# Keeping the residual in memory during the experts, so that its buffer can serve the weight ring

## The reference, cut to what matters

```
x  = x + g1 * mixer(...)                         # the residual, 128-row tiles
h2 = modulate(rmsnorm(x, norm_ffn_g), sh2, sc2)  # the second norm
f  = hier_moe(h2)    # per row 2 of 32 experts: (silu(h @ w1[e]) * (h @ w3[e])) @ w2[e]
x  = x + g2 * f
```

## Time and profile before

| | us |
|---|---|
| median of 3 runs | 2064.95 (2058.71 to 2065.15) |
| the profiled execution, time | 2062.01 |
| its span | 2060.2 |
| PE busy | 1904.3 (92%) |
| in the chain that ended last: PE, DMA | 66%, 22% |
| DMA RG<-in_moe_w in that chain | 20% |
| mean rate over the span | 287 GB/s |

### The profile page before, as it was taken

One profiled execution on the slowest core, in us unless ns is written; L12 is line 12 of the kernel. 1 busy time (PEld: TensorE's weight loads), 2 busy tenths in 40 slices (PEclk: granted clock), 3 DMA queues, 4 the chain that ended last, 5 costly groups with the idle time before them and its releaser, 6 DMA issues.

```text
span 2060.2 us, 35307 instructions
## 1 busy us (share of the span) xinstructions
PE 1904.3 (92%) x15271; PEld 1238.8 (60%) x15271; DVE 764.3 (37%) x1664; ACT 356.4 (17%) x795; POOL 307.4 (15%) x256
## 2 busy tenths in 40 slices
PE   6988999999999989999899888888789989999998
PEld 3565565555556548646555444444369779775884
DVE  1334382222222235315421111111157537647752
ACT  3132420000000012114210000000020130132231
POOL 0134411000000000116210000000000060040120
PEclk9999999999999999999999999999999999999999
DMA  9695399999999989318499999999975424417221
GB/s 331 174 330 216 106 392 389 427 427 426 427 425 424 426 336 308 109 41 318 169 371 427 426 427 426 426 426 425 420 283 179 144 80 164 145 61 205 83 94 61
DMA packets 136115, 591.02 MB, mean 287 GB/s; under 512 B 19410, under 2 KB 35818, under 8 KB 111248
## 3 DMA queue, kind: packets, MB, share of 16 engines
q1 hardware_dynamic: 119536, 564.45, 69.6%
q10 hardware_dynamic: 10304, 17.83, 2.8%
q0 software_dynamic: 6112, 6.39, 0.9%
HBM read 576.95 MB, written 25.33 MB: 292 GB/s over the span
## 4 chain that ended last, share of the span: by engine, by line
PE 66%; DMA 22%; DVE 5%; issue 3%; POOL 2%; ACT 2%; ACTq 0%; SPq 0%; DVEq 0%; POOLq 0%
DMA RG<-in_moe_w 20%; PE banks L1725 13%; PE banks L1007 7%; PE banks L1750 6%; PE banks L1270 4%; PE banks L1701 4%; PE banks L1010 4%; PE banks L2405 3%; PE banks L3093 3%; PE banks L3311 3%; PE banks L2862 2%; PE banks L720 2%; POOL AR L965 2%; PE banks L662 1%; PE banks L2864 1%
## 5 line engine op out<-in xcount | busy, mean ns | idle before, releaser
L1725 PE MATMUL banks<-RG,HT 128*64 128x256 f32 x3616 | 426.4, 389 | 38.5 <-DMA RG<-in_moe_w 36.2
L1725 PEld LDWEIGHTS banks<-RG,HT 128*64 128x64 f32 x3616 | 251.8, 134 | 224.8 <-DMA RG<-in_moe_w 60.2
L1734 DVE TENSOR_TENSOR AR<-AR,banks 128x256 f32<-128x256 f32 x64 | 38.6, 603 | 481.6 <-ACT AR L1730 430.4
L2004 POOL DMA_INDIRECT y_rows<-AR x64 | 63.7, 995 | 839.9 <-DVE AR L1764 811.7
L1750 PE MATMUL banks<-RG,AR 128*64 128x512 f32 x752 | 171.7, 598 | 3.8 <-DVE AR L1743 3.1
L1730 ACT ACTIVATE AR<-banks 128x256 f32<-128x256 f32 x64 | 24.5, 383 | 744.9 <-PE banks L1725 744.9
L1701 PE MATMUL banks<-AR 128*128 128x256 bf16 (+1 forms) x1152 | 149.4, 277 | 2.0 <-DVE AR L1689 1.5
L1701 PEld LDWEIGHTS banks<-AR 128*128 128x128 bf16 x1152 | 108.5, 98 | 33.6 <-issue 18.3
L1750 PEld LDWEIGHTS banks<-RG,AR 128*64 128x64 f32 x752 | 49.9, 136 | 94.4 <-issue 83.5
L1270 PE MATMUL banks<-RG,HT 128*128 128x512 f32 x192 | 84.8, 602 | 4.8 <-DVE AR L413 3.0
L965 POOL TENSOR_SCALAR AR<-AR,ST 128x768 f32<-128x768 f32 (+1 forms) x24 | 44.9, 1883 | 276.5 <-DVE ST L943 276.2
(11 more groups left out here) (508 smaller groups left out, 2766.3 us busy)
## 6 DMA issues: line engine op xcount, KB each, us to landing
RG<-in_moe_w SPq DMA_DIRECT2D x160, 2048.0 KB
AR<-in_moe_w SPq DMA_DIRECT2D x32, 2048.0 KB, 14.4
RG<-in_ada_w SPq DMA_DIRECT2D x24, 2048.0 KB
RG<-in_attn_w_in SPq DMA_DIRECT2D x20, 2048.0 KB
RG<-in_odd_w_in SPq DMA_DIRECT2D x6, 2048.0 KB
RG<-in_ssm_w_in SPq DMA_DIRECT2D x4, 2048.0 KB
AR<-y_rows SPq DMA_DIRECT2D x12, 512.0 KB, 6.2
RG<-in_even_w_out SPq DMA_DIRECT2D x2, 2048.0 KB
```

The source lines that it names most:

```text
L1725: m = pe.matmul(p[64 * h:64 * h + 64, 256 * i:256 * i + 256], x[:, k, :], w[:, h, k], start=k == 0, stop=k == 7, skip_group_check=True)
L2004: g.indirect_dma_start(y, off, E.Y[b], None, bounds_check=2047, oob_is_err=False).then_inc(*event)
```

## The change

- ACT stores each residual tile to a new DRAM tensor `x_rows` right behind the root of its second norm (`act_x_store`): four stores of 512 KB in layer 0, two in layer 1.
- `XS` becomes slot NS + 2 (7) of the ring. Before its first use in a layer SP waits for the last x store to have landed and for the last half of the norm.
- Slots are always put back, so slot 6 is used all through layer 1's experts. It enters as the second slot there and SP waits for the end of the attention and the second norm's gains before its first use.
- The order of the slots becomes 1, 2, 3, 4, 0, 7, 5 in layer 0 (seven) and 2, 6, 3, 4, 0, 7, 1, 5 in layer 1 (eight). Slot 7 is taken out when expert 30 is entered.
- Behind the issue of w2 of expert 31 SP waits for slot 7's last user and loads the residual back (`sp_x_back`), four or two loads of 512 KB. DVE's first `dve_last` waits for the last of them.
- `GATE1` moves from `XS` tile 3 to the small buffer `SVT`.

```diff
-    "mods_store0": ("x_loads",),
+    "mods_store0": ("x_loads", "x_back"),
...
+        XD = nc.dram_tensor("x_rows", [2, 512, D], F).ap()
...
-        extra = [None, ar(6 * KK, 4096)]
+        extra = [None, ar(6 * KK, 4096), XS[:].rearrange("p a b -> p (a b)")]
...
             slot = free.popleft()
-            if slot <= NS:
-                free.append(slot)
+            free.append(slot)
...
             extra[0] = ar((13, 11)[l] * KK, 4096)
-            free.insert(5, NS)
+            free.append(NS)
+            free.insert(5 - l, NS + 2)
             if l == 1:
-                free.insert(5, NS + 1)
+                free.insert(1, NS + 1)
...
+                if e == 30:
+                    free.remove(NS + 2)
...
+        def act_x_store(act, E, t):
+            act.dma_start(XD[E.l, 128 * t:128 * t + 128], XS[:, t, :]).then_inc(*dm("x_store", E.l, t))
+
+        def sp_x_back(sp, E, ended):
+            sp.wait_ge(*at(*ended))
+            for t in range(E.nt):
+                sp.dma_start(XS[:, t, :], XD[E.l, 128 * t:128 * t + 128]).then_inc(*dm("x_back", E.l, t))
...
                 act_root(act, (E.name, t), at_=t)
+                act_x_store(act, E, t)
                 act.wait_ge(*at(norm_end(E.name, t), E.name, t))
...
             act_root(act, (E.name, last), at_=last)
+            act_x_store(act, E, last)
             act_store_split(act, E, last - 1)
...
             v.wait_ge(*at("last_out", E.l, t))
+            if t == 0:
+                v.wait_ge(*at("x_back", E.l, E.nt - 1))
...
+                if slot >= NS + 1 and (key[1], slot) not in begun:
+                    l = key[1]
+                    begun.append((l, slot))
+                    if slot == NS + 1:
+                        sp.wait_ge(*at("att_out", "odd", 15))
+                        sp.wait_ge(*at("ada_scale", 1, 0))
+                    else:
+                        sp.wait_ge(*at("x_store", l, (3, 1)[l]))
+                        sp.wait_ge(*at("normed_half", (E0, E1)[l].name, (3, 1)[l], 1))
...
                 before[slot] = ended
+                if key[0] == "w2" and key[2] == 31:
+                    sp_x_back(sp, (E0, E1)[key[1]], before[NS + 2])
```

More of the change, by code:

```diff
@@ L298, in build @@
                 piece(("w2", l, e), down_source(W[2][e]), 4, 1024, ("down", l, x))
-            over_slots[l] = list(free)
+            over_slots[l] = [slot for slot in free if slot <= NS]
             free.remove(NS)
@@ L351, in build @@
                  ((4, 0, 0), (3, 0, 1), (4, 1, 2), (3, 1, 3), (2, 1, 5), (2, 0, 6), (5, 0, 7), (5, 1, 8))}
-        mods1 = {(2, 0): XS[:, 2, :], (5, 0): XS[:, 3, :], (3, 0): HT[:, 0:4, 256:512], (4, 0): HT[:, 4:8, 256:512]}
+        mods1 = {(2, 0): XS[:, 2, :], (5, 0): SVF[:, 0:512], (3, 0): HT[:, 0:4, 256:512], (4, 0): HT[:, 4:8, 256:512]}
         AB1 = SVF[:, 0:512].rearrange("p (a b) -> p a b", a=4)
@@ L2177, in sp_overflow @@
             last = where[("w2", l, 31)][2]
-            ended = {ring[i][3]: ring[i][4] for i in range(last - 5, last + 1)}
+            ended = {ring[i][3]: ring[i][4] for i in range(last - 11, last + 1)}
             W = [I[w][l].rearrange("e (p k) n -> e p k n", p=128) for w in ("moe_w1", "moe_w3")]
@@ L2569, in build @@
         FG, PG1 = ar(20 * KK, D), ar(21 * KK, D)
-        GATE1 = XS[:, 3, 0:512]
+        GATE1 = mods1[(5, 0)]
         def act_final_loads(act, e):
```

## The result

The changed kernel takes 2051.0 us (6 runs, 2047.8 to 2052.0) against 2061.1 us for the kernel before in the same sitting (6 runs, 2058.4 to 2065.2): ratio 0.9948, 95% interval 0.9935 to 0.9962. Two more sittings with the same two kernels gave 0.9975 (0.9962 to 0.9989) and 0.9973 (0.9960 to 0.9986), with 12 runs of the changed kernel and 35 of the one before each. The plain mean of the three ratios is 0.9965, some 7 us. Only the first of the three is a gain of over 0.3%.

The account below looks back on a forecast made before the run. The prediction took the weight stream to bound both expert stages; 3.9 us in layer 0 plus 4.3 in layer 1 gave 8.2, taking the median from 2065.0 to 2056.8 us, with an 8-in-10 range of 2051.5 to 2064.

Parts of the forecast that it names:

- The stream bounds both expert stages: Both layers' experts: each stage ends when the stream of 96 weight pieces ends, at about 426 GB/s.
- Layer 0, 3.9 us: Layer 0's experts: slot 7 closes two pauses, 4.5 us, less 0.6 for stores; below PE's 6.6 us of waits.
- Layer 1, 4.3 us: Layer 1: early piece and eight slots gain 4.3 us (3.3 to 4.9), with the x store landing after 11.1 us.
- one us for each us of later landing: Layer 1, SP before slot 7: each us the x store lands beyond 11.1 us costs one us.
- 4.9 us off the stream: Layer 1, before expert 0: slot 6's piece, issued at about 985 us, flows while nothing else does, saving 4.9 us.
- The way back, cost 0: Behind expert 31's w2: the residual's loads land 3 us before DVE needs them in layer 0; cost 0, at most 2 us.
- The traffic's cost: Stores beside the weights: the last x store costs 0.6 us in layer 0 and 1.2 us in layer 1.
- The number, 2056.8: Whole kernel: 8.2 us off the earlier runs' median of 2065.0 gives 2056.8 us.
- A: Layer 0: its lead is lost because PE bounds it, only layer 1's 4.3 us count; 2060.7 us, chance 0.17.
- B: Both layers: all twelve added transfers are paid in the stream, 14.8 us, net 3.1 us slower; 2068.1 us, chance 0.10.
- C: Layer 1: SP stands before slot 7 for the x store; gain gone at 19 us landing, 2072.7 at 27; chance 0.05.
- D: Start of layer 0's experts: more slots also bridge rate dips, gain above the sum; 2052 us, chance 0.06.

Follow-up runs that it names:

- slot6_only: Changed kernel without slot 7 and its stores, waits and loads in either layer; slot 6 still second and kept in layer 1; ratio 1.0006 to the kernel before.
- slot1_first: Changed kernel with slot 1 ahead of slot 7 in layer 1; ratios 0.9961 and 0.9967 to the kernel before.
- slot6_late: Changed kernel with slot 6 behind slot 7 instead of second in layer 1; ratio 0.9979 to the kernel before.
- layer0_only: Changed kernel with slot 7, its stores and loads in layer 0 alone, layer 1's ring as before the change; ratio 0.9979 to the kernel before.
- traffic_only: Kernel before's ring plus only the residual's stores and loads back, no slot 7, slot 6 for one piece; ratio 0.9997 to the kernel before.
- stores_ahead: Changed kernel with four more 512 KB stores ahead of layer 1's last x store; ratio 0.9997 to the kernel before.
- back_twice: Changed kernel with the residual loaded back twice, one after the other, DVE waiting for the second; ratio 1.0025 to the kernel before.

## Why the prediction was right and where it was wrong

**The stream bounds both expert stages: right.** Where pauses were closed and none opened (both layers of the changed kernel), the stage became shorter by about their sum. Where the pause only moved (slot6_only, slot1_first), or a store's data took its place (slot6_late), the stage from its first matmul on changed by 1.5 us at most.

**Layer 0, 3.9 us: right.** Measured 480.5 - 476.8 = 3.7 us over two profiles of before and three of after; 4.3 by the ratio of layer0_only. The working through two pauses of 1.4 and 3.1 us was borne out pause by pause. PE's waits before 460 us went, 3.4 of the 6.6 us of room.

**Layer 1, 4.3 us: right in sign and near in size, in part by luck.** Measured 470.8 - 465.6 = 5.3 us from expert 0's first matmul, 526.5 - 521.8 = 4.7 from the end of the attention. The landing of the x store, 12.4 us, was worse than the 11.1 taken, yet the pause there, 1.8 us, was less than the 2.1; slot 5 followed 3.2 us behind slot 7 and not 7, since the h store landed soon after. By the prediction's own price, one us for each us of later landing, a landing of 12.4 leaves 4.3 - 1.3 = 3.0 us. So that price was too high, and the term came within 0.4 to 1.0 us of the measured only because the landing had been taken too short as well. "4.9 us off the stream" for the early piece does not hold for that piece by itself: slot 6 alone gave 1.5 or 2.7 us in the profile and nothing in the timed runs. Without slot 7 the ring holds no eighth piece to flow when expert 0 starts. The prediction's sum counted both at once, as the change has both.

**The way back, cost 0: right,** with 1.5 us of slack in layer 0 where 3 were worked out. The traffic's cost (0.6 us in layer 0, 1.2 in layer 1) was not above what can be measured.

**The number, 2056.8: wrong, and the range missed by 0.5 us.** The mechanism gave 8.2 us; the stretches add up to 8.4 to 9.0; the three ratios give 10.7, 5.1 and 5.6. What failed is the last step, "from that the median becomes 2056.8". It takes the gain off a median of three runs, 2064.95. With 6 runs that median was 2061.1, with 35 it was 2057.9 in two sittings and 2058.3 in a third. The base was some 4 to 7 us too high, nearly as much as the whole gain, and the range allowed for scatter about that base only. The profiled execution was to take 2053.8 and took 2047.8; its start alone was 6.2 us earlier. Taken off 2057.9 to 2061.1, the forecast gain gives 2049.7 to 2052.9; the changed kernel took 2051.0, 2051.7 and 2051.0. Why the first sitting's ratio is lower than the two others' isn't settled; its 6 runs a side are few, and a start-up that moves by 7 us from run to run in the profiles can make such a difference. Nor is it settled why the two larger sittings time less than the stretches show: their intervals are 2.3 to 7.8 and 2.9 to 8.2 us. The profiles show no loss elsewhere. From layer 0's last addition to the attention's end both kernels take 223.1 to 223.6 us, and behind layer 1's last addition the one before took 551.2 and 549.7 us, the changed one 550.1, 547.7 and 552.0.

**The rivals.** A fell by layer0_only, B by traffic_only. C's wait is real (SP did stand 12.4 us, and the stream paused 1.8 us of it), but its threshold was not reached, and its price of one us for each us was not borne out: stores_ahead made the stand 5.8 us longer and the pause less than 1. D, more than the sum, is not shown by the stretches.

## What to carry to other kernels

In a stage bound by a load stream, look for the stretches in which the stream pauses and count how many pieces are out when the first slot comes free. One more slot pays if there is an idle stretch for its piece to flow in, and an idle stretch if the ring holds one piece more. Try the two together: from expert 0's first matmul on, each alone gained 1.5 us or nothing here, and both 5. Room for a slot may be found in a buffer that nobody reads for the whole stage, as long as its stores fall where the stream is idle and its way back fits behind the last piece. The 1.5 us of slack here are little: when the landing came later than that (back_twice), the excess stood in full as a wait of DVE.

## What the hardware showed that was not expected

A 512 KB store landed in 2.6 us in an idle stretch. Beside the weights the x stores took 7.3 to 12.4 us, and the h stores behind them on ACT's queue up to 15.8 us in the changed kernel and 18.2 in slot1_first, though the data of one is an estimated 1.2 us at 426 GB/s. Four stores more ahead of the last x store made its landing 16.4 us instead of 12.4 and SP's wait 5.8 us longer, little more than their data's 4.9 us. A second load of 2.1 MB, issued when the first had landed, let DVE start 9.2 us later, for 4.9 us of data, with the y rows beside it. The granted clock from 20 to 170 us varied between 0.97 and 1.00 from one execution to the next, and with it the first 185 us by up to 7.
